# Two transformer blocks on one core: first norm by rows, last taps on TensorE, sums by fours, memory norm early, mixer statistics parted

## The reference, cut to what matters

```python
a = modulate(rmsnorm(h, norm1_g[0]), sh1, sc1)        # shifts and scales come from c @ ada_w
u = a @ w_pw1 + b_pw1
x1, g = split(u)
v = dwconv(x1 * sigmoid(g), w_dw, b_dw)               # 31 taps along the tokens, each channel by itself
v = silu(layernorm(v, ln_g, ln_b))                    # mean and variance over 1024 channels
y = v @ w_pw2 + b_pw2
...
proj = rms_norm(x, mix_norm_g) @ w_in                 # second block
mkv  = rms_norm(mem, mem_norm_g) @ w_mem_kv           # 256 memory tokens
...
y = rwkv7_scan(r, w, k, v, -kk, kk * a)               # recurrence over 512 tokens, 6 heads of 64
y = (y - mean(y)) * rsqrt(var(y) + GN_EPS) * ln_w + ln_b
```

## Time and profile before

| | us |
|---|---|
| median of 3 runs (lowest, highest) | 2404.7 (2402.0, 2411.1) |
| profiled run | 2403.9 |
| its span | 2402.0 |
| PE busy | 2247.3 (94%) |
| DVE busy | 1300.6 (54%) |
| ACT busy | 1055.2 (44%) |
| POOL busy | 940.1 (39%) |
| granted TensorE clock, mean | 0.964 |

### The profile page before, as it was taken

The page is one execution under the profiler, slowest core; times in us unless marked ns, Lnnn a source line. Parts: engine busy times, 40 slices in busy tenths (PEclk is TensorE's granted clock), DMA queues, the critical chain, the costliest instruction groups (busy, mean ns, idle before and its releaser), DMA issues.

```text
span 2402.0 us, 37360 instructions
## 1 busy us (share of the span) xinstructions
PE 2247.3 (94%) x14219; PEld 1869.9 (78%) x14219; DVE 1300.6 (54%) x2203; ACT 1055.2 (44%) x1840; POOL 940.1 (39%) x551
## 2 busy tenths in 40 slices
PE   4999599999999999999989999979988889999998
PEld 4888487899999986777778888867746777778777
DVE  4699727736563745388433223457566536441441
ACT  5666545425442534388344234444454223431431
POOL 1799324435554624200254444433302113444443
PEclk9999798999999998999989999999989989999999
DMA  8788012212222212100123323333200003332332
GB/s 275 255 265 272 20 53 71 62 53 69 77 67 66 75 45 84 54 1 1 53 88 96 105 88 96 105 94 88 75 1 2 2 2 93 91 104 81 96 101 83
DMA packets 337940, 204.82 MB, mean 85 GB/s; under 512 B 6701, under 2 KB 335991, under 8 KB 337783
## 3 DMA queue, kind: packets, MB, share of 16 engines
q1 hardware_dynamic: 332747, 194.03, 26.9%
q10 hardware_dynamic: 5036, 8.66, 1.1%
HBM read 200.47 MB, written 2.19 MB: 84 GB/s over the span
## 4 chain that ended last, share of the span: by engine, by line
PE 48%; issue 19%; POOL 7%; DVE 3%; ACT 2%; DVEq 1%; ACTq 0%; POOLq 0%
PE ps L665 10%; PE ps L666 10%; PE ps L667 10%; POOL w_lo L590 6%; PE ps L2193 4%; PE ps L2194 4%; PE ps L2195 4%; PE ps L2513 1%; PE ps L3544 1%; PE ps L2541 1%; ACT w_hi L633 0%; PE ps L3512 0%; PE ps L3540 0%; POOL w_lo L616 0%; PE ps L3529 0%
## 5 line engine op out<-in xcount | busy, mean ns | idle before, releaser
L590 POOL TENSOR_TENSOR w_lo<-raw,w_hi 128x1024 fp32r<-128x1024 f32 (+3 forms) x202 | 488.7, 2420 | 1008.3 <-ACT w_hi L633 992.4
L665 PE MATMUL ps<-x_hi,w_hi 128*128 128x512 f32 (+1 forms) x1304 | 490.7, 376 | 29.7 <-DVE x_lo L1527 12.4
L666 PE MATMUL ps<-x_lo,w_hi 128*128 128x512 f32 (+1 forms) x1304 | 476.8, 366 | 0.0
L667 PE MATMUL ps<-x_hi,w_lo 128*128 128x512 f32 (+1 forms) x1304 | 475.9, 365 | 0.0
L633 ACT ACTIVATE w_hi<-raw 128x1024 fp32r<-128x1024 f32 (+3 forms) x230 | 244.7, 1064 | 508.2 <-PE ps L667 502.2
L665 PEld LDWEIGHTS ps<-x_hi,w_hi 128*128 128x128 f32 x1304 | 252.0, 193 | 86.5 <-issue 22.7
L666 PEld LDWEIGHTS ps<-x_lo,w_hi 128*128 128x128 f32 x1304 | 252.4, 194 | 40.6 <-issue 3.8
L667 PEld LDWEIGHTS ps<-x_hi,w_lo 128*128 128x128 f32 x1304 | 251.9, 193 | 38.7
L665 PE MATMUL ps<-g_hi,w_hi 128*128 128x512 f32 (+1 forms) x704 | 257.5, 366 | 3.5 <-POOL w_lo L590 1.4
L666 PE MATMUL ps<-g_lo,w_hi 128*128 128x512 f32 (+1 forms) x704 | 255.9, 363 | 0.0
L667 PE MATMUL ps<-g_hi,w_lo 128*128 128x512 f32 (+1 forms) x704 | 255.4, 363 | 0.0
(11 more groups left out here) (436 smaller groups left out, 4173.9 us busy)
## 6 DMA issues: line engine op xcount, KB each, us to landing
raw<-in_ffn_w_up SPq DMA_DIRECT2D x52, 512.0 KB, 3.7
ada_tail<-in_ada_w SPq DMA_DIRECT2D x22, 1024.0 KB, 8.1
raw<-in_w_up SPq DMA_DIRECT2D x44, 512.0 KB, 3.7
ada_s<-in_ada_w SPq DMA_DIRECT2D x20, 1024.0 KB, 8.0
zq<-in_ffn_w_up SPq DMA_DIRECT2D x72, 256.0 KB, 2.8
raw<-in_conv_w_pw SPq DMA_DIRECT2D x24, 512.0 KB, 6.2
raw<-in_ffn_w_down SPq DMA_DIRECT2D x16, 704.0 KB, 4.4
raw<-in_w_down SPq DMA_DIRECT2D x16, 704.0 KB, 4.4
```

The source lines that it names most:

```text
L590: pool.tensor_tensor(M.w_lo[:, slot, 0:K * P], M.raw[:, slot, 0:K * P], M.w_hi[:, slot, 0:K * P].bitcast(F32), ALU.subtract).then_inc(lo_r ...
L665: pe.matmul(o, wh, hi[:, k, t0:t0 + tn], start=first, stop=False)
L666: pe.matmul(o, wh, lo[:, k, t0:t0 + tn], start=False, stop=False)
L667: return pe.matmul(o, wl, hi[:, k, t0:t0 + tn], start=False, stop=last)
```

## The change

1. n10 sums into six rows of 128 tokens, one pair of ada products earlier, and uses the layer norm's small root, reciprocal and spreading. `ada_dve` moves behind the first two t, and VectorE makes pw1's first two low parts there.
2. VectorE's last addition of a slice adds the bias and writes `cv`; ScalarE's copy is gone. VectorE waits for it and drains ahead of freeing the pair. For slice 7 TensorE does nine more taps into a pair of its own, ScalarE and GpSimd 11, VectorE 10. The mods' transposes move behind the mean.
3. The layer norm's squares get eight buffers; GpSimd adds two pairs, VectorE two, TensorE sums four. The root's table is loaded ahead.
4. Two slices of memory per chunk m of down11 are transposed and split (m below 4), the memory's statistics are made at m = 5 and 6, and three high parts of weights move forward.
5. In the mixers' loop `variance` is cut into `centred` (e = 3) and the rest (e = 4, behind the state), with `deviation` at e = 5, and `turned` comes behind the tokens' transposes.

```diff
@@ -947,8 +952,10 @@
     def ada_pe(pe):
...
         for n in range(0, ADA_FIRST, 2):
+            if n == ADA_FIRST - 4:
+                norm_pe(pe, "n10")
             if n == ADA_FIRST - 2:
-                norm_pe(pe, "n10")
+                rows_back_pe(pe, "n10")
@@ -1005,6 +1012,31 @@
...
+    def last_taps_pe(pe):
+        pe.wait_ge(diag_last, 1)
+        pe.wait_ge(gate_ready, done(KD))
+        for n in range(LAST_TAPS):
+            tap = PE_TAPS + n
+            for t0, t1, at in ((0, SEQ, VLAT), (SEQ, TOK, VCTX)):
+                mm = pe.matmul(M.pair(2, t0, t1), M.diag_last[n],
+                               M.vp[:, 7 % 3, at - PAD + tap:at - PAD + tap + t1 - t0], start=(n == 0),
+                               stop=(n == LAST_TAPS - 1))
+        mm.then_inc(last_taps, 1)
+    def diag_last_act(act):
+        for n in range(LAST_TAPS):
+            c = COL["conv_w_dw"] + (PE_TAPS + n) * 8 + 7
+            ins = act.activation(M.diag_last[n], ident, ACT.Identity, scale=M.prm[:, c:c + 1], bias=0.0)
+        ins.then_inc(diag_last, 1)
+    def last_copy_act(act):
+        act.wait_ge(tap_done, conv_done(6))
+        act.wait_ge(last_taps, 1)
+        act.activation(M.pc[:, 0, :], M.pair(2), ACT.Copy).then_inc(last_copy, 1)
@@ -1032,7 +1064,7 @@
...
                 ada(n)
-        turn_mods_pe(pe)
+        last_taps_pe(pe)
@@ -1102,12 +1134,21 @@
...
     def norm_pe(pe, name):
-        i, pair, w = NN[name], norm_pair(name), NORM_W[name]
+        i = NN[name]
...
         pe.wait_ge(sq_used, done(7 * i + 7))
-        for t0, tn in (BOTH if w == TOK else LAT):
-            mm = pe.matmul(M.pair(pair, t0, t0 + tn), ones, M.n_t[:, 0, t0:t0 + tn], start=True, stop=True)
+        for b in range(6):
+            mm = pe.matmul(stat_rows(name), M.pick6[:, 5 - b:11 - b], M.n_t[:, 0, b * P:(b + 1) * P],
+                           start=(b == 0), stop=(b == 5))
...
+    def rows_back_pe(pe, name):
+        pe.wait_ge(ln_rt, done(NN[name] + 1))
+        for b in range(6):
+            mm = pe.matmul(M.pair(norm_pair(name), b * P, (b + 1) * P), ident[0:6, b:b + 1].to_broadcast([6, P]),
+                           ln_row(0), start=True, stop=True)
+        mm.then_inc(ln_back, 1)
@@ -1347,12 +1388,19 @@
...
         if stream == "down11":
-            if m < KD:
-                act.wait_ge(mem_t, done(m + 1))
-                act.activation(M.h[:, m, SEQ:TOK], M.pair(m % 4, SEQ, SEQ + CTX), ACT.Copy).then_inc(mem_ready, 1)
+            if m < 4:
+                for k in (2 * m, 2 * m + 1):
+                    act.wait_ge(mem_t, done(k + 1))
+                    act.activation(M.h[:, k, SEQ:TOK], M.pair(k % 4, SEQ, SEQ + CTX), ACT.Copy).then_inc(mem_ready, 1)
+            if 1 <= m <= 4:
+                parts_act(act, MEMO, 2 * m - 2)
+                parts_act(act, MEMO, 2 * m - 1)
+            if m == KD:
+                high(act, "mem_kv", 0, 0)
             if m:
-                parts_act(act, MEMO, m - 1)
                 parts_act(act, MIX, m - 1)
+            if m == 6:
+                memo_stats_act(act)
@@ -1360,8 +1408,12 @@
...
         if stream == "down11" and m:
-            parts_dve(dve, MEMO, m - 1)
+            if m <= 4:
+                parts_dve(dve, MEMO, 2 * m - 2)
+                parts_dve(dve, MEMO, 2 * m - 1)
             parts_dve(dve, MIX, m - 1)
+            if m == 6:
+                memo_stats_dve(dve)
@@ -1480,17 +1532,18 @@
...
                 ln_square_act(act, k)
-            ln_root_act(act)
+            root_table(act)
+            ln_root_act(act, name)
...
                     square_act(act, name, k)
-            act.wait_ge(stat_ready, done(i + 1))
-            act.activation(M.n_y[:, 0, 0:w], M.pair(pair, 0, w), ACT.Sqrt, scale=1.0 / D, bias=eps_col)\
-                .then_inc(rms_ready, 1)
+            if name == "n10":
+                group_act(act, 0, 0, 0)
+                root_table(act)
+            ln_root_act(act, name)
         if name == "n10":
-            for g in (0, 1):
-                group_act(act, g, 0, g * 1024)
+            group_act(act, 1, 0, 1024)
@@ -1529,9 +1575,19 @@
...
             dve.tensor_tensor(M.n_t[:, k % 2, 0:w], M.pair(pair, 0, w), src, ALU.mult).then_inc(t_ready, 1)
+            if name == "n10" and k == 1:
+                ada_dve(dve)
+                for q in (0, 1):
+                    weight_low_dve(dve, q)
...
+    def weight_low_dve(dve, q):
+        dve.wait_ge(hi_ready, done(q + 1))
+        dve.tensor_tensor(M.w_lo[:, q, 0:KD * P], M.raw[:, q, 0:KD * P], M.w_hi[:, q, 0:KD * P].bitcast(F32),
+                          ALU.subtract).then_inc(lo_ready, 1)
@@ -1588,7 +1644,23 @@
...
     DVE_TAPS = TAPS - PE_TAPS - POOL_TAPS
-    NEXT_AT = 12
+    NEXT_AT = (12, 12, 12, 12, 12, 12, 11)
...
@@ -1610,10 +1682,10 @@
...
-            for i in range(DVE_TAPS):
-                if i == NEXT_AT and j < 7:
+            for i in range(dve_taps(j)):
+                if j < 7 and i == NEXT_AT[j]:
                     gated(j + 1)
-                tap = PE_TAPS + POOL_TAPS + i
+                tap = first_tap(j) + pool_taps(j) + i
@@ -1623,9 +1695,16 @@
...
                         .then_inc(tap_done, 1)
-            dve.wait_ge(tap_done, done((2 * DVE_TAPS + 1) * (j + 1) - 1))
-            dve.wait_ge(pool_tap, done(SUMS * (j + 1)))
-            dve.tensor_tensor(M.pair(j % 2), M.pc[:, j % 2, :], M.pair(j % 2), ALU.add).then_inc(tap_done, 1)
+            if j == 7:
+                dve.wait_ge(tap_done, conv_done(j) - 2)
+                dve.wait_ge(last_copy, 1)
+                dve.tensor_tensor(M.pair(1), M.pc[:, 0, :], M.pair(1), ALU.add).then_inc(tap_done, 1)
+            dve.wait_ge(tap_done, conv_done(j) - 1)
+            dve.wait_ge(pool_tap, done(SUMS * j + pool_taps(j) - 1))
+            dve.scalar_tensor_tensor(out=M.cv[:, j, :], in0=M.pc[:, j % 2, :], scalar=M.col("conv_b_dw", j),
+                                     in1=M.pair(j % 2), op0=ALU.add, op1=ALU.add).then_inc(tap_done, 1)
+            dve.wait_ge(tap_done, conv_done(j))
+            dve.drain().then_inc(evac, 2)
@@ -1680,45 +1759,38 @@
...
         for j in range(8):
+            if j == 7:
+                diag_last_act(act)
...
                 weights(2 * j + 4)
-            if j:
-                copy_conv(act, j - 1)
             groups_to(pairs_of(j)[1])
-            for n in range(5, POOL_TAPS):
+            for n in range(5, pool_taps(j)):
...
                 tap_act(act, j, n)
+        last_copy_act(act)
...
         mods_back_act(act)
-        copy_conv(act, 7)
-    def copy_conv(act, j):
...
     def mean_pe(pe):
         pair = Q0["pw2"] % 4
-        pe.wait_ge(evac, done(Q0["pw2"] - 4))
+        pe.wait_ge(evac, done(Q0["pw2"] - 2))
         for k in range(KD):
-            pe.wait_ge(cv_ready, done(k + 1))
+            pe.wait_ge(tap_done, conv_done(k))
...
@@ -1728,35 +1800,48 @@
...
+        for k in (0, 2, 4, 6):
+            if k < 4:
+                pe.wait_ge(ln_sum_p, k // 2 + 1)
+            else:
+                pe.wait_ge(ln_sum, k // 2 - 1)
...
+                mm = pe.matmul(stat_rows("ln"), M.pick6[:, 5 - b:11 - b], ln_square(k)[:, b * P:(b + 1) * P],
+                               start=(k == 0 and b == 0), stop=(k == 6 and b == 5))
+        mm.then_inc(stat_ready, 1)
+        rows_back_pe(pe, "ln")
+    def ln_square(k):
+        return (M.n_sq, M.n_t, M.n_y, M.ln_last)[k // 2][:, k % 2, :]
+    def ln_sums_pool(pool):
+        for k in (0, 2):
+            pool.wait_ge(sq_ready, done(8 * NN["ln"] + k + 2))
+            pool.tensor_tensor(ln_square(k), ln_square(k), ln_square(k + 1), ALU.add).then_inc(ln_sum_p, 1)
+    def ln_sums_dve(dve):
+        for k in (4, 6):
+            dve.wait_ge(sq_ready, done(8 * NN["ln"] + k + 2))
+            dve.tensor_tensor(ln_square(k), ln_square(k + 1), ln_square(k), ALU.add).then_inc(ln_sum, 1)
     def ln_square_act(act, k):
...
+        act.activation(ln_square(k), M.cv[:, k, :], ACT.Square).then_inc(sq_ready, 1)
@@ -1779,11 +1864,13 @@
...
                 diag_pool(pool, j + 1)
-            for n in range(8, POOL_TAPS):
+            for n in range(8, pool_taps(j)):
...
                 low_stream(pool, "pw1", 2 * j + 5, 2 * j + 6)
-        low_stream(pool, "pw2", 0, 8)
+        low_stream(pool, "pw2", 0, 2)
+        ln_sums_pool(pool)
+        low_stream(pool, "pw2", 2, 8)
@@ -2952,8 +3039,12 @@
     def down11_pe(pe):
         for m in range(8):
-            mem_turn_pe(pe, m)
+            if m < 4:
+                mem_turn_pe(pe, 2 * m)
+                mem_turn_pe(pe, 2 * m + 1)
             products(pe, "down11", m // 4, m % 4, LAT, HALF * 4)
+            if m == 5:
+                memo_stats_pe(pe)
@@ -3031,15 +3122,17 @@
     def w_in_pe(pe):
         q0 = Q0["w_in"]
-        memo_stats_pe(pe)
         pe.wait_ge(MEMO.x, done(KD))
+        pe.wait_ge(mix_sd, done(1))
...
                 products(pe, "w_in", p // 4, p % 4, LAT)
-            if p - 1 < 8:
+            if p == 2:
```

(23 more changed lines are left out.)

113 lines of the change are left out of this document (50 added, 63 removed).

## The result

| | before | after |
|---|---|---|
| median of 4 runs, us | 2404.7 (2402.0 to 2411.1) | 2376.1 (2374.7 to 2380.6) |
| profiled run, its span, us | 2403.9, 2402.0 | 2377.3, 2375.5 |
| mean granted clock of TensorE | 0.964 | 0.972 |

The account below looks back on a forecast made before the run. TensorE was taken as the bound nearly everywhere (busy 94% of the span). Terms of -1.75 + 1.8 - 12 - 9.7 - 2.5 = -24.2 us gave 2380.5 us on the median of 2404.7, range 2370 to 2391.

Parts of the forecast that it names:

- First norm: Start of pw1: reciprocal off the path, two weight lows on VectorE; TensorE begins at 48.8 for 50.55, -1.75 us.
- Slices: Eight convolution slices: VectorE's fused last add and wait cost 0.3 us a slice, six times, +1.8 us.
- End of the convolution: Last slice: nine diagonal taps on TensorE; the mean ends at 259.9 to 261.8 for 270.5, -10.6 to -8.7 us.
- case of late data: End of the convolution: the last ada pair doesn't move up; diagonal taps start at 240.0, not 238.1.
- Sums: Layer norm statistics behind the mean: TensorE's groups fall from eight to four, -2.5 us.
- Memory: Memory's norm and split moved under down11: -6.3 up to w_in's chunk 1, -3.4 behind it, -9.7 us, range -12 to -6.
- the ring: Two-buffer weight ring replaces the norm's wait: 3.6 us per mem_kv chunk; w_in's chunk 1 at 1600.5 for 1606.82, -6.3.
- Mixers: Mixers' loop: half the variance behind level 4 saves 5.1, less waits for x0 and a longer VectorE queue; -2.5 us.
- (a): Memory: the weight ring doesn't let early memory pay, each mem_kv chunk waits; only 3.4 of 9.7 left, 2386.8; chance 0.12.
- (b): Mixers' norm turns into equal waits, last ada pair late, first lows at GpSimd's price: 2386.3; chance 0.10.
- (c): End of the convolution: last taps on TensorE run at low clock behind a pause, 10.6 lost, 2391.1; chance 0.06.
- (d): Slices: fused add and next tap each lose two GpSimd sums, 7.7 us a slice, 2440; chance 0.03.

Follow-up runs that it names:

- five groups: Kernel after, but TensorE takes squares 0 and 1 singly and GpSimd adds only 2 and 3, five groups of sums for four: 2373.5 us, 0.9879 of the kernel before.

## Why the prediction was right, point by point

- **First norm, -1.75; -1.6 measured, by luck.** Two steps failed, in opposite directions. "Takes the same 1.9 us" is wrong: 1.44 of that were the operations on 128x8, held by GpSimd's lows, which went to VectorE. They take 0.24 now, and from mods to the product are 4.39 us for 6.31. And "its row transposes end at 43.26" held only where TensorE had its full clock: in the trace after they end at 44.58, 1.3 later, since the edit made TensorE's own queue the path to them and that queue ran at half clock. Where it didn't, pw1 began at 47.67, so the part is worth 2.9 at full clock and 1.6 or less at half.
- **Slices, 0.3 each; 0.41 measured.** Mechanism right (a wait in VectorE's queue), size low; and it does not show in the end, since the cover is TensorE's chain. The GpSimd contention that I kept as the upper bound doesn't occur.
- **End of the convolution, right:** nine taps 11.88 for 11.5; full clock; slice 7 at 258.86 for 257.9. That TensorE's chain, begun by the last ada pair, decides and not VectorE stood there as the case of late data (starting at 240.0); it is between the two, 238.88.
- **Sums, -2.5; -1.9.** The wait for GpSimd's sum and a low clock at the first group were in the sum, which had the end 11.9 behind the mean. It is 12.45: not one group but two run at half clock (0.53 in 265.8 to 270.8).
- **Memory, -9.7; -9.0.** The ring sets the pace as said: mem_kv's chunks start 3.9, 3.4 and 5.4 us behind each other. The term that was mis-sized is "+0.3" for the turn with a busy GpSimd: from chunk 2 to 3 are 5.35 for 3.6, 1.75 more. Behind the ring the step gave 0.5 more.
- **Mixers, -2.5; -3.3** between the marks. VectorE's waits of 1.5 us are gone, none of them is over 0.5 now, and the wait that was estimated for the last x0 at 1.4 is there with 1.29. TensorE's idle time fell by 3.1 and its busy time didn't, so the mechanism is the waits, as forecast.
- **Left out:** the clock in stretches without an edit, -2.4. The forecast took every such stretch as unchanged. The other steps between the marks add up to -24.2, as forecast, which is luck in part: slices, sums and the ring gave less than forecast, mixers, down11 and the step behind the ring more. The span fell by 2.3 more than the sum of 24.2. The other 2.0 of the 4.4 us between the forecast and 2376.1 lie in the profiled runs: that of before is 0.8 below its median, that of after 1.2 above.
- **Rivals.** (a) appears in small (2.22, by another queue's order). (b) doesn't: the waits in the mixers are fewer, the last ada pair starts without waiting, at 236.99, and a low costs 1.18. (c) and (d) don't: clock 1.00, a slice 0.41 longer and not 3.3.
- **The bounds.** The forecast's lower bound of -31 is mis-added: -24.2, -1.8 for the drain, -2.3 for the ring and -4.5 for the mixers make -32.8. The measured -28.6 is inside both.

None of the variants is shown to beat the changed kernel: the lowest median, 2373.5 of five groups, has an interval that covers its.

## What to carry to other kernels

Ask of an added operation in whose queue it waits, not only how long it lasts: a copy of 0.9 us that waits 5 us on ScalarE starved GpSimd and cost 2.6 us at the end, while 0.41 us a slice on a full VectorE cost next to nothing, because the stage ended on TensorE. A long pause of TensorE costs its length and also the half clock behind it, here 1.4 to 3.1 us more. To tell waits from clock, compare idle and busy time over the whole way between two marks: a stretch of 10 us picked from it can show a gain of clock that the whole way doesn't have. And when an edit puts work ahead of something in TensorE's queue, ask what that work takes at half clock too: here 1.3 to 2.6 us of pw1's start hung on it.

## What was unexpected of the hardware

- An operation of VectorE on 128x8 with two inputs in SBUF was held 2.1 us by a GpSimd operation that had begun 0.06 us earlier (2.38 for 0.24).
- Stretches at half clock lie elsewhere when work hundreds of microseconds earlier is changed: the second attention, without an edit, took 56.2 to 59.1 us from mark to mark, the way from ahead of the loop to w_out, with the same order, 175.5 to 179.3, and the same kernel gave the same value twice (56.50 and 56.49). The cause is open.
- The same pause of 6.85 us was followed by a clock of 0.61 for four microseconds in one kernel, and by 0.50 and 0.66 for eight in another, so how long the low clock lasts was not the pause's doing alone.
